# Expert weights on two issuing queues: the down weights go to ScalarE's queue

## What is computed

```python
def expert_block(args):
    xb, e = args
    return (jax.nn.silu(xb @ w_gate[e]) * (xb @ w_up[e])) @ w_down[e]

ys = lax.map(expert_block, (xs, block_e)).reshape(n_slots, d)
ys = ys * slot_gate[:, None].astype(ys.dtype)
return jax.ops.segment_sum(ys, slot_tok, num_segments=n + 1)[:n]
```

## Time and profile before

| | us |
|---|---|
| median of 3 runs | 1376.86 (1376.77 to 1377.25) |
| the profiled execution | 1376.48 |
| its span, first to last instruction | 1374.5 |
| PE busy in the span | 1251.7 (91%) |
| all DMA, share of 16 engines' time (largest queue) | 85.9% |
| expert loop of layer 0, first down product to last combine | 354.0 to 797.7 |
| expert loop of layer 1, the same | 924.9 to 1365.8 |

### The profile page before, as it was taken

The page is one execution under the profiler, slowest core; times in us unless marked ns, Lnnn a source line. Parts: engine busy times, 40 slices in busy tenths (PEclk is TensorE's granted clock), DMA queues, the critical chain, the costliest instruction groups (busy, mean ns, idle before and its releaser), DMA issues.

```text
span 1374.5 us, 13838 instructions
## 1 busy us (share of the span) xinstructions
PE 1251.7 (91%) x5118; PEld 519.0 (38%) x5118; DVE 391.1 (28%) x844; ACT 210.0 (15%) x441; POOL 69.9 (5%) x86
## 2 busy tenths in 40 slices
PE   6999989888999998898988899899999999888896
PEld 3445544544433333232332266453333333322232
DVE  4387655526211111111211034451121112111112
ACT  2312115611111111010101011111111011010010
POOL 0123000000000000000000000000000000000000
PEclk9999989999999999999999999999999999999999
DMA  9958678464799999999999993539999999999994
GB/s 356 372 226 338 234 273 304 185 247 190 285 421 422 422 423 422 421 422 422 422 422 422 418 381 159 208 123 391 421 422 422 422 422 422 422 422 422 422 422 189
DMA packets 83265, 486.55 MB, mean 354 GB/s; under 512 B 6176, under 2 KB 7712, under 8 KB 34080
## 3 DMA queue, kind: packets, MB, share of 16 engines
q1 hardware_dynamic: 81216, 481.91, 85.9%
q10 hardware_dynamic: 2016, 4.21, 0.9%
HBM read 485.04 MB, written 1.05 MB: 354 GB/s over the span
## 4 chain that ended last, share of the span: by engine, by line
PE 59%; SPq 19%; DMA 12%; DVE 6%; issue 2%; ACT 2%; POOL 0%; POOLq 0%; ACTq 0%; DVEq 0%
PE PS L740 19%; SPq L289 14%; DMA ring<-in_moe_w_up 10%; PE PS L759 10%; PE PS L578 8%; PE PS L767 5%; SPq L294 4%; PE PS L548 2%; PE PS L851 2%; PE PS L869 2%; PE PS L641 2%; PE PS L732 2%; DMA ring<-in_attn_w_in 2%; PE PS L460 1%; PE PS L605 1%
## 5 line engine op out<-in xcount | busy, mean ns | idle before, releaser
L740 PE MATMUL PS<-ring,KQH 128*64 128x512 f32 x2048 | 483.6, 616 | 35.0 <-DMA ring<-in_moe_w_up 33.3
L740 PEld LDWEIGHTS PS<-ring,KQH 128*64 128x64 f32 x2048 | 147.5, 141 | 316.3 <-issue 277.4
L759 PE MATMUL PS<-ring,KQH 128*64 128x512 f32 x1024 | 230.7, 592 | 0.9 <-ACT KQH L1048 0.9
L1532 DVE COPY TMP<-PS 64x512 f32<-64x512 f32 x64 | 43.7, 683 | 472.4 <-PE PS L759 472.4
L759 PEld LDWEIGHTS PS<-ring,KQH 128*64 128x64 f32 x1024 | 73.7, 137 | 146.9 <-issue 145.5
L767 PE MATMUL PS<-TMP,KQH 128*128 128x512 f32 x256 | 118.4, 605 | 1.6 <-DVE TMP L1532 1.6
L578 PE MATMUL PS<-ring,KQH 128*128 128x512 f32 x256 | 116.6, 599 | 0.0
L1035 ACT COPY TMP<-PS 64x512 f32<-64x512 f32 x64 | 37.2, 581 | 468.0 <-PE PS L759 468.0
L1547 DVE TENSOR_TENSOR KQH<-KQH,PS 128x256 f32<-128x256 f32 x64 | 38.7, 605 | 196.3 <-ACT KQH L1054 196.2
L415 POOL COPY KQH<-KQH 128x512 f32 x62 | 38.1, 614 | 864.1 <-PE PS L740 776.4
L767 PEld LDWEIGHTS PS<-TMP,KQH 128*128 128x128 f32 x256 | 46.0, 189 | 73.6 <-issue 70.3
(11 more groups left out here) (224 smaller groups left out, 796.4 us busy)
## 6 DMA issues: line engine op xcount, KB each, us to landing
ring<-in_moe_w_gate SPq DMA_DIRECT2D x128, 1024.0 KB, 26.9
ring<-in_moe_w_up SPq DMA_DIRECT2D x128, 1024.0 KB, 26.8
ring<-in_moe_w_down SPq DMA_DIRECT2D x64, 2048.0 KB, 28.8
ring<-in_ada_w SPq DMA_DIRECT2D x24, 2048.0 KB, 15.5
ring<-in_attn_w_in SPq DMA_DIRECT2D x2, 4096.0 KB, 12.8
ring<-in_attn_w_in SPq DMA_DIRECT2D x2, 2048.0 KB, 21.2
ring<-in_attn_w_out SPq DMA_DIRECT2D x1, 4096.0 KB, 15.0
ring<-in_pool_w_in SPq DMA_DIRECT2D x1, 4096.0 KB, 25.1
```

What stands on the lines that cost most here:

```text
L740: ins = mm(PS[64 * f:64 * f + 64, 4, :], xs[:, k, 0:SLOTS], gu_w[s][:, :, k, 256 * f:256 * f + 256], start=k == 0, stop=k == KC - 1)
L759: ins = mm(PS[64 * f:64 * f + 64, 6, :], lhs, dn_w[s][:, c, 512 * f:512 * f + 512], start=c == 0, stop=c == 3)
L1532: return V.tensor_copy(y_sb[64 * second:64 * second + 64, 0:512], PS[0:64, 6, :])
```

## The change

The down weights of experts 3 to 31 are no longer issued by SP. ACT issues them, in step e for expert e + 3, right after its copy L1035 of expert e's down product. That copy waits for `dn_done` of expert e, which is the condition that SP waited for. Experts 0 to 2 of each layer are loaded as before, and no transfer changes its size. PE's program is the same. ACT's loop has four turns of six experts instead of five, and the last eight experts are written out, so that the last three steps issue nothing.

```diff
                 if freed:
-                    sp.wait_ge(L.dn_done, e - 2)
+                    return
                 sp.dma_start(dn_rows[s], w_down[L.l, e].rearrange("(a p b) n -> p a b n", a=2, b=2)).then_inc(L.dn_in[s], 16)
...
                     act.wait_ge(L.dn_done, e + 1)
                     upper_outputs(c % 2).then_inc(L.y_a, 1)
+                    if not isinstance(e, int) or e + 3 < NE:
+                        s = L.slot(c)
+                        act.dma_start(dn_rows[s], w_down[L.l, e + 3].rearrange("(a p b) n -> p a b n", a=2, b=2)
+                                      ).then_inc(L.dn_in[s], 16)
                     if not last:
...
-                with act.Fori(0, TURNS) as it:
+                with act.Fori(0, TURNS - 1) as it:
                     for c in range(BODY):
                         step(BODY * it + c, c)
-                step(BODY * TURNS, 0)
-                step(BODY * TURNS + 1, 1, last=True)
+                for e in range(BODY * (TURNS - 1), NE):
+                    step(e, e, last=e == NE - 1)
```

## The result

| | before | after |
|---|---|---|
| median, us (9 runs each) | 1376.77 (1374.46 to 1379.27) | 1383.24 (1379.99 to 1385.59) |
| ratio to before, 95% interval | | 1.0047 (1.0036 to 1.0058) |
| the profiled execution, us | 1376.48 | 1385.59 |
| its span, us | 1374.5 | 1383.8 |

The changed kernel is slower by 6.5 us, 0.47%. The forecast was 1385.0, in a range of 1380.0 to 1392.0. The profiled execution of after is the longest of its nine, so its difference to before (9.1 us) is more than that of the medians.

The account below looks back on a forecast made before the run. The weight stream's DMA rate was taken to bound the expert loops. Per layer, an earlier start (-3.4 us) and a longer end net +4.0 and +4.1, ACT's issues 0: 1376.86 + 8.1 = 1385.0 us, range 1380.0 to 1392.0.

Parts of the forecast that it names:

- The stream is bytes over rate: Middle of the expert loops: DMA always busy at 422 GB/s, 14.9 us per expert, so order cannot change the stream's length.
- Start: Start of each layer's expert stream: expert 4's first half no longer stands behind SP's down wait; -3.4 us per layer.
- How the two queues share: Expert loops: SP's and ACT's queues take turns one to one, so ACT's 2 MB down transfer lands some 13 us after issue.
- End: Last experts: more PE work left after the last landing; net of the earlier start, +4.1 us layer 1, +4.0 layer 0.
- E': Time at which a layer's last weights land in the changed kernel, forecast to be the second half of expert 31.
- The sum: Both layers' expert loops together: 8.1 us added to the median of 1376.86, giving 1385.0 us.
- the clock's: PE's clock in expert 30's first half, kept as before: halved in layer 0, full in layer 1; halving costs 2.4 us.
- The bound with the full clock in both: Ends of both layers with PE at full clock in expert 30's first half: 1.6 + 4.1 = 5.7 us, 1382.6 in all.
- ACT's issues at nothing: ACT's 29 more issues a layer fall in its pause before the silu: 0 us; if they block, at most +1.5 per layer.
- SP's issues would fall to 0.4 us: SP's issues in the expert loops, before blocking up to 8.31 us, take 0.4 us each with 8 MB at most queued.
- Landing in order of issue: Rival: ACT's transfers queue behind SP's, so earlier issue is all gain at the loops' ends; 1363.0 us, chance 6%.
- slower mixed stream: Rival: mixing two queues lowers the expert loops' DMA rate; +51 us (1436), chance 4%, or +8 (1393), chance 5%.

Follow-up runs that it names:

- the first experiment: Against the kernel before: all weights stay on SP's queue, issued in the order in which slots come free; 1363.23 us, ratio 0.9903.
- the wait kept: Against the changed kernel: SP still waits for dn_done of expert e - 3 after the second half of e, issuing nothing there; 1388.83 us.
- the end on SP: Against the changed kernel: down of experts 28 to 31 issued by SP with its old wait, ACT keeping 50 of 58 transfers; 1369.28 us.
- The kernels above: The follow-up kernels, each timed beside the kernel before; without the two that cut down across partitions, from 1363.23 to 1395.33 us.
- only 30 and 31 on ACT: Against the kernel before: down of experts 30 and 31 alone issued by ACT, 4 of 58 transfers; 1395.33 us, ratio 1.0134.

## Why the prediction held, point by point

**The stream is bytes over rate.** It held: 422 GB/s in after as before. From the start of the first down product to the last landing, layer 1 took 1356.6 - 930.0 = 426.6 us, where it took 1354.9 - 924.9 = 430.0. On one queue, in the first experiment, it took 426.6 as well.

**Start, -3.4 us per layer.** That difference is 3.4 us, and 3.6 in layer 0. Two experiments took it away and laid it bare: 5.6 us lost over two layers with the wait kept, and -7.4 with the end on SP, against 6.8 each. These totals hold some of the clock too. The table's column "stream" does not.

**How the two queues share.** The prediction names one 512 KB load of ACT. There were two, and the packets that it counts from 56 to 58 us are of the second, since the first had landed at 56.0:

```profile
48.92 0.82 ACTq L927 DMA_DIRECT2D TMP<-in_ada_b  x2
```

The reading stands even so, and it held for transfers of another size and packet: from 1335 to 1345 us, while one down transfer was under way in layer 1, the two queues of after moved

```profile
q1 hardware_dynamic: 293, 2.13, 51.2%
q10 hardware_dynamic: 272, 2.10, 50.3%
```

(packets, MB, share of the engines), so one to one, and the whole engine set full. Down landed 13.9 us after its issue in the median, and 13 was forecast.

**End.** Layer 1: down of 31 at E' + 10.3, as worked out. From the start of the first down product to that of the last it took 1366.97 - 929.97 = 437.0 us where it had taken 1357.66 - 924.9 = 432.8: +4.2, forecast +4.1. Layer 0, the same: 793.41 - 354.54 = 438.9 against 789.56 - 354.00 = 435.6: +3.3, between the bounds of +1.6 and +4.0. In both layers of after the clock fell once near the end, and in layer 0 not where I had put it. In layer 0 it was the second half of expert 30 that had to wait and took 5.35 us:

```profile
762.52 3.65 PE L740 MATMUL PS<-ring,KQH 128*64 128x512 f32 x16 [0.69 <-DMA ring<-in_moe_w_up]
766.00 3.60 PE L759 MATMUL PS<-ring,KQH 128*64 128x512 f32 x16
771.53 5.35 PE L740 MATMUL PS<-ring,KQH 128*64 128x512 f32 x16 [1.92 <-DMA ring<-in_moe_w_up]
```

So down of 31 starts 12.0 us after the last landing there, where I had 10.1 with the full clock and 12.5 with a slow first half. The time lost is about right, but the event is another: that layer 0 came out so near is in part luck. In layer 1 the first half took 5.35 us, in the shadow of the second half's landing, and it cost nothing that shows. I had split PE's spare time as 0.5 us ahead of each second half and 2.3 ahead of the even first; the waits of these two experts, 0.69 and 1.92 in layer 0 and 1.00 and none in layer 1, fall differently from pair to pair.

**The sum.** In the profiled executions the two loops give 3.3 + 4.2 = 7.5 us of the forecast 8.1. Their spans differ by 9.3. The other 1.8 lie outside the loops: layer 0's loop starts 0.5 us later, and from the last down product of layer 0 to the first of layer 1 it takes 929.97 - 793.41 = 136.6 us and not 135.3. The kernels above had 134.9 to 137.0 there with no edit in that stage, so I don't count it to the change. The medians differ by 6.5, with an interval of 5.0 to 8.0: the term that was mis-sized is most likely the clock's. I took each layer as it had been and got 8.1. The bound with the full clock in both was 5.7, and the medians lie between. What speaks for it: of the nine executions of after, the longest (1385.59 us, the profiled one) had a mean granted clock of 0.976 over the span, and the two shortest (1379.99 and 1380.02) 0.984 and 0.983. Where in the kernel the others lost their clock, no trace shows.

**ACT's issues at nothing.** The issue rows of ACT show 0.37 to 0.40 us each, none blocked. The run with 50 of them kept its whole gain but for 1.9 us over both layers, and no run shows whether that is theirs.

**What was wrong.** I wrote that SP's issues would fall to 0.4 us, as 8 MB at most would stand in its queue. The median of the up issues fell from 2.1 to 0.7 us, but single ones still block, 7.38 us for the last. When the last one of layer 1 was issued, five halves, 10 MB, were under way ahead of it: gate and up are held back by the down weights, so more of them are under way than in my count. It cost nothing that the stream shows (426.7 us).

**The rivals.** Landing in order of issue was forecast at 1363.0, with a chance of 6%, and did not happen on two queues. It is just what the first experiment built on one queue, at 1363.23. The slower mixed stream did not appear, so the 338 GB/s window of the earlier trace rows is no price of two queues as such. The Trainium skill's sentence that issuing from several engines only saves the sequencer's time ("DMA: Bandwidth & Descriptors", Issuing engines are not separate DMA queues) describes the rate and not the order: the rate stayed at 422 GB/s, and the time moved by 6.5 us.

## What to carry to other kernels

In these loops, bound by a stream of weights, the order of issue hardly changed the stream's length, but it changed both ends. In such a stage, look for the first transfer that waits behind another one's condition, and count how much work is left for the compute engine after the last landing. A second queue takes its share at once, so put on it only what is needed first. What is needed last must land last. Here one queue in the order in which the slots come free did both, and was 1.0% faster than the kernel before and 1.4% faster than the change (1363.2 against 1376.7 and 1383.2 us).

## What was not expected of the hardware

Cutting a transfer into partitions 0 to 15 and 16 to 127 slowed the whole stream. On one queue it ran at 231 to 287 GB/s in windows of 100 us in the expert loops, with the 16 DMA engines busy, against 422, and the kernel took 1986.5 us. In the trace of the run with the first piece on ACT, packets of 8 KB took 0.54 us in the median, against 0.31 before. Why is open: no run varied where a piece starts or how many partitions it has by itself, so it may be either piece. Splitting along the rows of a partition had no such effect (420 GB/s).

TensorE's clock fell to half (1.2 GHz) in single stretches of a few us after waits for weights, and a group of 16 matmuls then took 5.0 to 6.7 us in place of 3.65. The length of the wait alone did not decide it. In the traces of before, after and the eight kernels near 422 GB/s it fell after waits of 0.7 to 6.1 us, and after others of up to 2.4 us it did not. One of each, in after and in the kernel with only 30 and 31 on ACT:

```profile
553.80 5.35 PE L740 MATMUL PS<-ring,KQH 128*64 128x512 f32 x16 [0.68 <-DMA ring<-in_moe_w_up]
```
```profile
1127.56 3.65 PE L742 MATMUL PS<-ring,KQH 128*64 128x512 f32 x16 [2.44 <-DMA ring<-in_moe_w_up]
```

In the middle of these loops, bound by DMA, the slower groups did not lengthen the stream: after has them and the first experiment has none, and their streams take 426.7 and 426.6 us in layer 1. They cost time in the last waits before it ended.
